# Sixteen extra matrix products at two idle places of TensorE in a two-layer streaming encoder step

## The reference

```
proj = x @ w_in                                     # one wide projection, split among the branches
A: latent attention from proj;  B: gated recurrence from proj
x = LN1(alpha*x + (sigmoid(ga)*(A @ w_br_a) + sigmoid(gb)*(B @ w_br_b)) @ w_out)
x = LN2(alpha*x + moe(x) + sigmoid(x @ w_ple_gate) * (ple @ w_ple))   # moe: top 2 of 32 experts
```

## Time and profile before

| | |
|---|---|
| time, median of 3 runs | 1840.06 us (1838.45 to 1840.39) |
| the profiled execution | 1842.88 us |
| its span, first to last instruction | 1841.1 us |
| PE busy | 1572.2 us, 85% of the span |
| PE's share of the chain that ended last | 67% |
| mean granted TensorE clock | 0.856 of full |

### The profile page before, as it was taken

The page is one execution under the profiler, slowest core; times in us unless marked ns, Lnnn a source line. Parts: engine busy times, 40 slices in busy tenths (PEclk is TensorE's granted clock), DMA queues, the critical chain, the costliest instruction groups (busy, mean ns, idle before and its releaser), DMA issues.

```text
span 1841.1 us, 21048 instructions
## 1 busy us (share of the span) xinstructions
PE 1572.2 (85%) x8984; PEld 825.6 (45%) x8985; DVE 450.1 (24%) x1007; ACT 268.0 (15%) x651; POOL 49.6 (3%) x95
## 2 busy tenths in 40 slices
PE   6999779998998788778698998799899987788773
PEld 3556554554453244423253665544545443244420
DVE  3231661152101111010313417511601101110003
ACT  2332321111000000000125323111110000000001
POOL 1200000000000000000021000000000000000000
PEclk9999888997968787788798998799878778877776
DMA  8302213446999999999842033043669999999992
GB/s 293 115 1 92 98 52 127 138 180 264 426 408 426 427 426 426 426 426 426 317 143 70 1 113 123 6 154 110 268 261 427 415 426 426 426 426 427 426 427 99
DMA packets 97458, 491.04 MB, mean 267 GB/s; under 512 B 9264, under 2 KB 15184, under 8 KB 47696
## 3 DMA queue, kind: packets, MB, share of 16 engines
q1 hardware_dynamic: 92608, 478.16, 63.8%
q0 software_dynamic: 4752, 11.45, 1.9%
HBM read 486.69 MB, written 2.89 MB: 266 GB/s over the span
## 4 chain that ended last, share of the span: by engine, by line
PE 67%; DMA 19%; DVE 7%; issue 3%; ACT 2%; SPq 1%; DVEq 0%; POOL 0%; ACTq 0%
PE bank L759 64%; DMA ring<-in_w_e_up 11%; DMA ring<-in_w_e_down 5%; PE bank L786 2%; DMA arena<-in_w_e_up 2%; SPq L627 1%; DVE arena L1774 1%; PE bank L1181 1%; DVE x_sb L1605 1%; DVE x_sb L1607 1%; DMA lnw<-in_ln_b 1%; DVE arena L1775 1%; DVE arena L1807 1%; DVE arena L1994 0%; ACT arena L1553 0%
## 5 line engine op out<-in xcount | busy, mean ns | idle before, releaser
L759 PE MATMUL bank<-arena 128*32 128x512 f32 (+12 forms) x2392 | 589.3, 526 | 185.0 <-DMA ring<-in_w_e_up 93.0
L759 PE MATMUL bank<-ring,arena 128*32 128x512 f32 (+4 forms) x1976 | 479.9, 616 | 4.2 <-ACT arena L1553 1.4
L759 PE MATMUL bank<-ring,xT 128*32 128x128 f32 (+5 forms) x2496 | 450.2, 397 | 4.6 <-ACT xT L1284 2.3
L759 PEld LDWEIGHTS bank<-arena 128*32 128x32 f32 (+7 forms) x2392 | 224.9, 154 | 503.0 <-issue 482.4
L759 PEld LDWEIGHTS bank<-ring,xT 128*32 128x32 f32 (+1 forms) x2496 | 222.0, 143 | 217.7 <-issue 198.8
L759 PE MATMUL bank<-arena,x_sb 128*128 128x128 f32 (+1 forms) x768 | 252.5, 478 | 11.0 <-DVE arena L1961 10.5
L759 PEld LDWEIGHTS bank<-arena,x_sb 128*128 128x128 f32 (+1 forms) x768 | 202.1, 327 | 68.2 <-issue 59.0
L759 PEld LDWEIGHTS bank<-ring,arena 128*32 128x32 f32 (+1 forms) x1976 | 136.0, 131 | 101.7 <-issue 93.9
L759 PE MATMUL bank<-cst,arena 128*32 128x512 f32 (+2 forms) x256 | 132.0, 656 | 0.0
L759 PE MATMUL bank<-lb,arena 128*32 128x512 f32 x160 | 90.3, 718 | 0.0
L759 PE MATMUL bank<-xT,arena 128*32 128x512 f32 x128 | 79.1, 776 | 0.0
(11 more groups left out here) (216 smaller groups left out, 832.2 us busy)
## 6 DMA issues: line engine op xcount, KB each, us to landing
ring<-in_w_e_up SPq DMA_DIRECT2D x66, 1024.0 KB, 24.6
ring<-in_w_e_down SPq DMA_DIRECT2D x60, 1024.0 KB, 26.0
arena<-in_w_e_gate SPq DMA_DIRECT2D x58, 1024.0 KB, 25.5
ring<-in_w_e_gate SPq DMA_DIRECT2D x50, 1024.0 KB, 26.7
arena<-in_w_e_down SPq DMA_DIRECT2D x48, 1024.0 KB, 25.8
arena<-in_w_e_up SPq DMA_DIRECT2D x44, 1024.0 KB, 23.4
ring<-in_w_in SPq DMA_DIRECT2D x32, 1024.0 KB, 8.6
cst<-in_w_e_gate SPq DMA_DIRECT2D x10, 1024.0 KB, 26.3
```

What stands on the lines that cost most here:

```text
L759: return pe.matmul(out, lhsT, rhs, start=first, stop=last, skip_group_check=True)
```

## The change

GpSimd first writes zeros to the first 512 columns of `xT` and raises a new semaphore `warm_in`. PE waits for it and multiplies this area by itself ten times (128 rows, 128 columns of weights, 512 columns) into bank 5. At the end of layer 0, after the last combining job and ahead of the waits for its readers, PE makes six such products on the constants. Nothing reads bank 5 in between, and the next job that uses it starts afresh.

```
+            pool.memset(xTw[:, 0:512], 0.0).then_inc(warm_in, 1)
             pool.memset(sm[:, :], 0.0).then_inc(zeroed, 1)
...
+            def warm(a, n):
+
+                for _ in range(n):
+                    mm(banks[5][:, :], a[:, 0:P], a, True, True)
+
             pe.sem_inc(more_matmuls, 1)
+            pe.wait_ge(warm_in, 1)
+            warm(xTw[:, 0:512], 10)
             pe.wait_ge(ident_in, 16)
             pe.wait_ge(eps_set, 1)
...
+                if layer < DEPTH - 1:
+                    warm(cst[:, 0:512], 6)
                 for job in COMBINE_JOBS:
                     job_read(pe, (layer, "moe", QUADS - 1) + job)
                 further_passes(pe, layer, turn, more)
```

More of the change, by code:

```diff
@@ L469, in build @@
         ident_in = sem("ident_in")
+        warm_in = sem("warm_in")
         ln0_in = sem("ln0_in")
```

## The result

The changed kernel takes 1842.83 us (median of 17 runs, 1839.5 to 1845.6), the kernel before 1839.37 us (17 runs, 1837.5 to 1840.4). The ratio is 1.0020 with a 95% interval of 1.0013 to 1.0028: about 3.7 us slower, where 3.6 us faster was predicted.

The account below looks back on a forecast made before the run. PE was taken as the bound (67% of the chain of waits), slowed by half clock after idling. 1842.88 - 2.9 (border) - 0.5 (head) - 0.2 (loads) = 1839.3 us profiled, 1836.5 us as a median; range 1833.0 to 1843.0 us.

Parts of the forecast that it names:

- The added products: Border: 12 rows at full clock, 5.16 us; head: 20 rows from 1.5 us, ending at 12.5 to 14.0 us.
- Nothing else: Both places: new wait and writes only on PE and GpSimd, no conflict with buffers or readers; no cost counted.
- Idle time of 1.05 us behind the six products: Border: PE idles 1.05 us instead of 6.23 before tile 0's transposes, short enough to keep the clock.
- The border's 2.9 us: Between the layers: saving from transposes and first products at full instead of half clock; bounds 2.0 and 3.5 us.
- the sign of being wrong that the prediction named: Border: the forecast is wrong if the clock is 0.50 in the first product of layer 1.
- Transposes keep the clock: Border: transposes, though thin work, leave the clock at 1.00; the contrary rival, 1839.2 us, had 10%.
- The head's 0.5 us: Kernel start: small saving, since the clock probably falls again in 2.1 to 3.6 us of idleness; bounds 0 and 3.34.
- GpSimd's loads: Head: clearing delays these loads by about 0.6 us, freeing the bias load: 0.2 us earlier, bounds 0.6 either way.
- The branch rival: Border: PE's register load waits for the six products, so its branch ends late; 1842.8 us, chance 18%.
- the 1.1 us that the prediction named as the sign: Border: if the forecast holds, PE's branch starts within 1.1 us of the end of the combining jobs.
- Savings kept to the end: After the border the chain hangs on PE, not loads, so savings reach the end in full.

Follow-up runs that it names:

- e3: The kernel before plus 65 semaphore increments on PE at its head that nothing waits for, no added products; 1842.86 us, ratio 1.0015.
- e5: The full change plus 20 semaphore increments on PE after the ten products of the head; 1839.61 us, ratio 0.9998 to the kernel before.
- e1: Head part alone: the full change without the six products at the border; 1841.18 us, ratio 1.0007 to the kernel before.
- e2: Border part alone: the full change without GpSimd's clearing, the wait and the head's ten products; 1839.04 us, ratio 0.9991 to the kernel before.
- e4: The full change plus 191 semaphore increments on PE after the ten products of the head; 1855.84 us, ratio 1.0080 to the kernel before.
- e6: The kernel before plus 90 semaphore increments on PE at its head; 1839.92 us, ratio 1.0001.
- e7: The kernel before plus only GpSimd's clearing of 512 columns, no products; 1840.75 us, ratio 1.0003.
- e8: The kernel before plus nine products at the border, no head part; 1835.55 us, ratio 0.9980.
- e11: The kernel before plus nine products at the border and 29 semaphore increments on PE at its head; 1840.51 us, ratio 1.0013.
- e12: The kernel before plus 41 semaphore increments on PE at its head; 1839.44 us, ratio 1.0003.
- e9: Head part alone (ten products, none at the border), with the clearing on VectorE instead of GpSimd; 1839.43 us, ratio 1.0002 to the kernel before.
- e10: The kernel before plus nine products at the border, thirteen at the head and the clearing on VectorE; 1837.75 us, ratio 0.9991.

## Why the prediction was wrong, step by step

- **The added products, 0.43 us a row, run at full clock from the end of the combining jobs.** Right: 12 rows in 5.42 us at the border. At the head, 20 rows ended at 12.5 us (12 to 14 predicted).
- **"Nothing else" changes: the failed step.** The prediction went through waits, buffers and readers, and left out that added instructions take places in a program which PE, by the packets of 16 KB in its trace, fetches block by block, and leaves by a jump. The 65 of them moved the target to about ten instructions ahead of the end of its block (an estimate from the count above), and the fetch of the next came into the open (913.09 to 914.05 us, in a break of 2.58 us), on the chain that sets the end. The prediction put this at nothing. Cost: 2.8 us for the shift alone (e3, 1.1 to 4.2), 4.0 us by change against e5 (1.0020 - 0.9998 of 1839 us; 2.7 us by the medians over before). What is left without it is about nothing: -0.4 us in e5, and -0.4 us by e1 and e2 together.
- **Idle time of 1.05 us behind the six products: mis-sized, 2.5 us.** It was taken from a profile in which tile 0 and the branch were ready within 0.2 us of each other. The branch ends 1.3 to 1.5 us after the packet with its target has landed, in all fourteen profiles. That packet starts late where the loads of layer 1 still fill the DMA engines. In nine profiles the DMA share is 1.04 to 1.06 in the first 0.9 us of the branch; there the packet starts 3.5 to 3.7 us after the branch, which takes 6.0 to 6.2 us (after, e1, e2, e4, e6, e7, e8, e11, e12). In five the share is 0.65 to 0.80; there it starts 1.0 to 1.9 us after, and the branch takes 3.6 to 4.4 us (before, whose 4.40 us are in the earlier trace rows, e3, e5, e9, e10). The order of the two is seen, that the one causes the other is inferred. In most profiles PE is then ready some 1.6 us after tile 0 (7.73 to 7.97 us idle in e1, e6, e7 and e12, against 6.23 us in the earlier trace rows). In e2 2.45 us of idleness cost the clock in the first products.
- **The border's 2.9 us (bounds 2.0 and 3.5):** 1.7 us from six products (e2; 0.2 us by the medians), 3.7 us from nine (e8). That products keep the clock was right (1.00 from 903.9 to 919.0 us in e8), six were too few (0.50 from 913.6 us on in e2). In the change itself the sign of being wrong that the prediction named did appear: the clock was 0.50 in the first product of layer 1.
- **Transposes keep the clock:** in e2 it was 1.00 through them (911.46 to 912.58 us) and fell at 913.5 us, behind them; with no gap ahead of them (e8) it stayed at 1.00 (911.7 to 919.0 us).
- **The head's 0.5 us:** the clock fell in the idle time, as said, and nothing is gained (e1, e9). What was overlooked is that the first products can't start before their weights land: 20.00 us in the change, 19.1 to 19.8 in e1, e5, e9 and e10, and 18.7 to 19.6 in the seven profiles with an untouched PE head or fillers only. In the earlier trace rows they started at 18.79 us and that wait did not show.
- **GpSimd's loads, 0.2 us earlier (bounds 0.6 either way):** the first load moved back by 0.27 us (1.61 against 1.34 us), not by 0.6, since the clearing took 0.53 us and a gap ahead of the load shrank. In time e7 gives +0.6 us with an interval of -0.9 to 2.2: neither size nor sign is shown.
- **The branch rival:** its price (1842.8 us) is nearly the time measured, and its mechanism is refuted: the register load did not wait for the products (904.8 us, beside products from 904.00 to 909.42 us). The branch starts 1.6 us after the end of the combining jobs, as it did before (907.36 and 908.95 us); the 1.1 us that the prediction named as the sign were misread from its own rows. The measured time lies inside the predicted range of 1833.0 to 1843.0 us only because this rival had widened it: a good number for a wrong reason, and luck. The rival named the right instruction and the wrong side of it. It asked what stands ahead of the branch, and not how much of the block is left behind its target.
- **Savings kept to the end:** shown for the border as far as e8 goes (3.7 us, with an interval of 2.0 to 5.1, where the profile of before had 3.47 us to be won); for the head not (e10).

## What to carry to other kernels

Where a long program has a jump that is taken, count the instructions added ahead of its target, useful or not: here 65 that do nothing cost 2.8 us (e3), and for 41 (e12) and 90 (e6) no cost is shown (0.6 us with an interval of -1.1 to 2.2, and 0.2 us with -1.3 to 1.8). Test such a change also with a few dozen no-op instructions, or its time may be that of the shift. An idle time named "issue" with one packet of the instruction queue in it was the sign (2.58, 1.42 and 2.12 us in after, e3 and e11). When filling an idle time to keep the clock, size the filling by when the engine is really ready, over several executions, and not by the one profile at hand: six products left 2.45 us idle and the clock fell (e2), nine left no gap and it stayed at 1.00 (e8). And a saving ahead of a stage that is bound by loads has to be shown behind that stage: the 1.65 us by which tile 1 of the head is ahead in e10 show in the time of no run.

## What the runs showed of the hardware

- A taken branch on PE costs 3.3 to 6.2 us here, against 0.06 to 0.07 us on VectorE. With quiet DMA engines (the end of layer 1 in the profile of before, share 0.02) it takes 3.41 us. In the change, at a share of 1.05, it takes 6.16 us: 3.7 us from its start to that of the 16 KB packet (905.66, 909.32), 1.07 us of packet, and 1.4 us behind it.
- The next block's packet starts 3.2 to 3.9 us after the first, and PE goes on 1.2 to 1.3 us after it has landed (after: 914.05, 915.24; e3: 914.51, 915.74; e11: 912.83, 914.15).
- In the change PE's register load and branch started at 904.8 and 905.7 us, beside products that stand ahead of them in its program and ran from 904.00 to 909.42 us.
- A semaphore increment by PE took about 0.1 us of issue (e4: 191 in 19.5 us).
- Under products of zeros with unread results the clock rose: at the head of the change their weight loads stand 0.86 us apart up to 5.75 us and 0.43 us apart from 6.34 us on, and the record has 1.00 from 6.06 us. Under products of constants with unread results it stayed: 1.00 through the border in e8 (903.9 to 919.0 us).
